# ScalarE's order during the residual update: embedding copies moved behind two tiles' act_hi

## The reference

```python
x = x + rmsnorm(y, norm_post[i])
gate = jax.nn.sigmoid(rmsnorm(x, pe_norm[i]) @ pe_w_gate[i])
x = x + gate * (p[i] @ pe_w_proj[i])
```

## Time and profile before

| | |
|---|---|
| median of 3 runs | 659.37 us |
| the profiled execution: its own time | 658.61 us |
| its span, first to last instruction | 656.8 us |
| TensorE busy | 635.0 us (97%) |
| VectorE, ScalarE, GpSimd busy | 389.9, 321.2, 308.1 us |
| chain that ended last | TensorE 81%, VectorE 9%, ScalarE 4% |
| mean granted clock of TensorE | 0.997 |

### The profile page before, as it was taken

One profiled execution on the slowest core, in us unless ns is written; L12 is line 12 of the kernel. 1 busy time (PEld: TensorE's weight loads), 2 busy tenths in 40 slices (PEclk: granted clock), 3 DMA queues, 4 the chain that ended last, 5 costly groups with the idle time before them and its releaser, 6 DMA issues.

```text
span 656.8 us, 9280 instructions
## 1 busy us (share of the span) xinstructions
PE 635.0 (97%) x2930; PEld 516.4 (79%) x2930; DVE 389.9 (59%) x776; ACT 321.2 (49%) x556; POOL 308.1 (47%) x412
## 2 busy tenths in 40 slices
PE   6979999999999999899989999999999999999897
PEld 3758888888888887788767778888888887887686
DVE  5528787867878787645678735333423343365864
ACT  6536575755656575465547633212222222465461
POOL 1765555556464445200277647547454752001770
PEclk9989999999999999999999999999999999999999
DMA  6253333332433333135002413232223232250041
GB/s 200 88 174 128 127 106 105 104 105 104 129 118 114 111 129 125 33 128 188 6 33 72 150 53 110 98 125 96 96 68 123 96 128 87 94 173 32 33 128 65
DMA packets 27161, 68.69 MB, mean 105 GB/s; under 512 B 3568, under 2 KB 10096, under 8 KB 27136
## 3 DMA queue, kind: packets, MB, share of 16 engines
q1 hardware_dynamic: 27136, 68.37, 31.6%
HBM read 66.23 MB, written 2.13 MB: 104 GB/s over the span
## 4 chain that ended last, share of the span: by engine, by line
PE 81%; DVE 9%; ACT 4%; issue 3%; DMA 2%; SPq 0%; DVEq 0%; ACTq 0%
PE ps_pj L1028 23%; PE ps_pj L1030 23%; PE ps_pj L1029 23%; PE ps_tr L1037 3%; DVE act_lo L918 2%; DMA w_raw<-in_weights 2%; PE ps_o L1141 1%; PE ps_o L1142 1%; DVE xT L914 1%; PE ps_sc L1111 1%; PE ps_sc L1109 1%; PE ps_tr L1028 1%; PE ps_tr L1030 1%; PE ps_tr L1029 1%; ACT logit L524 1%
## 5 line engine op out<-in xcount | busy, mean ns | idle before, releaser
L408 POOL TENSOR_TENSOR w_lo<-w_raw,w_hi 128x256 fp32r<-128x256 f32 x324 | 251.5, 809 | 138.5 <-ACT w_hi L468 128.3
L1028 PE MATMUL ps_pj<-act_hi,w_hi 128*128 128x512 f32 (+1 forms) x736 | 293.9, 399 | 5.5 <-DVE act_lo L918 4.4
L1030 PE MATMUL ps_pj<-act_hi,w_lo 128*128 128x512 f32 (+1 forms) x736 | 286.2, 389 | 0.0
L1029 PE MATMUL ps_pj<-act_lo,w_hi 128*128 128x512 f32 (+1 forms) x736 | 285.9, 388 | 0.0
L1028 PEld LDWEIGHTS ps_pj<-act_hi,w_hi 128*128 128x128 f32 x736 | 138.8, 189 | 37.2 <-DVE act_lo L918 7.9
L1030 PEld LDWEIGHTS ps_pj<-act_hi,w_lo 128*128 128x128 f32 x736 | 138.5, 188 | 29.3
L1029 PEld LDWEIGHTS ps_pj<-act_lo,w_hi 128*128 128x128 f32 x736 | 139.0, 189 | 24.9 <-issue 0.7
L468 ACT CAST w_hi<-w_raw 128x1024 fp32r<-128x1024 f32 x96 | 100.6, 1048 | 97.4 <-DMA w_raw<-in_weights 74.9
L443 POOL TENSOR_TENSOR acc<-acc,sq 128x512 f32<-128x512 f32 x14 | 21.4, 1525 | 118.5 <-ACT sq L616 117.6
L416 POOL TENSOR_TENSOR bias<-bias,future 128x128 f32<-128x128 f32 x64 | 34.0, 562 | 72.8 <-DMA bias<-negc_scratch 72.8
L524 ACT ACTIVATE logit<-logit,nmax 128x128 f32<-128x128 f32 (+1 forms) x64 | 36.1, 564 | 60.4 <-DVE nmax L763 60.2
(11 more groups left out here) (143 smaller groups left out, 724.8 us busy)
## 6 DMA issues: line engine op xcount, KB each, us to landing
w_raw<-in_weights SPq DMA_DIRECT2D x100, 512.0 KB, 3.4
bias<-negc_scratch SPq DMA_DIRECT2D x16, 256.0 KB, 7.4
bias<-negc_scratch SPq DMA_DIRECT2D x16, 192.0 KB, 6.1
xT<-in_xT SPq DMA_DIRECT2D x8, 256.0 KB, 5.5
bias<-negc_scratch SPq DMA_DIRECT2D x16, 128.0 KB, 4.8
out<-xT SPq DMA_DIRECT2D x7, 256.0 KB, 2.0
bias<-negc_scratch SPq DMA_DIRECT2D x16, 64.0 KB, 3.4
p_in<-in_pT SPq DMA_DIRECT2D x2, 512.0 KB, 4.5
```

Of the source, the lines that this page charges most:

```text
L408: last = nc.gpsimd.tensor_tensor(w_lo[place % RING][:, tiles], w_raw[stream(place) % RAW][:, tiles], w_hi[place % RING][:, tiles], ALU.sub ...
L1028: nc.tensor.matmul(out, w_h, a[0][:, k, tokens], start=k == first, stop=False)
L1029: nc.tensor.matmul(out, w_h, a[1][:, k, tokens], start=False, stop=False)
L1030: end = nc.tensor.matmul(out, w_l, a[0][:, k, tokens], start=False, stop=k == last)
```

## The change

The first copy of an embedding tile leaves its place ahead of the loop, and all four copies of a layer are placed by the table: tile 0 after act_hi 1, tile 1 after act_hi 2, tiles 2 and 3 after act_hi 3. The other engines' programs are as they were.

```diff
-PLE_COPY_AT = {0: [1], 1: [2, 3]}
+PLE_COPY_AT = {1: [0], 2: [1], 3: [2, 3]}
...
                     nc.scalar.copy(pleT[:, m, :], ps_pj[s % 2][:]).then_inc(pj_free[s % 2], 1)
 
-                ple_copy(0)
                 for m in range(KT):
                     act.wait_ge(x_new, 2 * KT * l + m + 1)
                     nc.scalar.activation(a_g[:, m, :], xT[:, m, :], ACT.Copy, scale=g_pe[:, l, m:m + 1]
```

## The result

The changed kernel takes 654.02 us (median of 4 runs, 652.78 to 654.84) against 659.35 (median of 4 runs of the kernel before, 658.58 to 660.58). The two medians are 5.3 us apart; the ratio estimated from the same runs is 0.9912 with a 95% interval of 0.9888 to 0.9936, which is 5.8 us less (4.2 to 7.4). Measured once more, the ratio is 0.9933 (0.9915 to 0.9951), 4.4 us less.

A forecast was written before the change was run, and what follows sets the result against it. Matmuls bound the kernel nearly everywhere; only the gate stage, where TensorE waits for VectorE's act_lo, had something to give. 2 x 2.1 = 4.2 us off the median of 659.37 gave 655.2 us, range 653.9 to 657.4.

The forecast's parts named there:

- Step 1: ScalarE: act_hi 0 and 1 go ahead at no cost, act_hi 0 at 317.22, copy 0 still at 319.36.
- Step 2: VectorE: act_lo 0 starts at 318.42 rather than 320.60, 2.18 us sooner.
- Step 3: GpSimd: additions start near 320.55, slowing VectorE; act_lo 1 takes 1.1 us, xT 3 1.0, ending at 323.15.
- late bound of 324.0: VectorE: end of xT 3 if act_lo 1 takes 1.78 us and xT 3 1.21, the whole early overlap paid.
- Step 4: PSUM banks: copies 2 and 3 free them later; first gate product at 324.55, 1.36 us later, second-bank stop gone.
- Step 5: act_lo 6 ends at 337.0 as TensorE reaches tile 6; TensorE ends at 341.25, gaining 2.1 us a layer.
- Step 6: Later stages: TensorE is full there, so the shift is passed on whole; 2 x 2.1 = 4.2 us.
- A: Banks cost more: xT 3 at 324.0, TensorE starts at 325.4; gain 1.5 us a layer, 656.4 us; chance 0.14.
- B: No gain: GpSimd slows VectorE to a 3.40 us pitch, act_lo 6 ends at 339.1 as before; 659 us; chance 0.07.
- C: Slower: VectorE's pitch reaches 3.65 us, act_lo 6 ends 1.3 us later than now; 662.0 us; chance 0.03.
- E: Edit without effect: act_hi 0 on ScalarE finds another hold than copy 0; 659.4 us; chance 0.02.
- Rival D: TensorE's clock: the new 1.3 us idle lowers it for 3 us, losing 1.5 us a layer; 658.2 us; chance 0.04.

The follow-up runs named there:

- experiment 5: Kernel before, with GpSimd's additions of squares cut to one of 512 columns (output not the reference's): ratio 0.9888, stage 26.42 us in both layers.
- experiment 7: Changed kernel with copy 2 ahead of act_hi 3 and GpSimd's additions cut to one of 512 columns: ratio 0.9901, stage 26.69 and 26.67 us.
- experiment 1: The changed kernel measured again without any edit: ratio 0.9933 to the kernel before, stage 27.70 and 27.65 us.
- experiment 4: Kernel before, with copy 0 left first, copy 1 behind act_hi 2, copies 2 and 3 behind act_hi 3: ratio 1.0077, stage 32.30 and 30.68 us.
- experiment 9: Kernel before's copy places, but squares behind ScalarE's last act_hi and additions on VectorE behind its last act_lo: ratio 0.9966, stage 28.07 and 28.44 us.
- experiment 3: Changed kernel with copy 0 behind act_hi 0, copy 1 behind act_hi 1, copies 2 and 3 behind act_hi 2: ratio 0.9937, stage 28.23 and 28.19 us.
- experiment 2: Changed kernel with copy 2 moved ahead of act_hi 3: ratio 0.9904 to the kernel before, stage 26.99 and 27.03 us.

## Why the prediction was wrong

The direction and the mechanism were right; the number was not. 655.2 us was forecast with a range of 653.9 to 657.4. The measured ratio, put on the median of 659.37, is 653.6 (652.0 to 655.2), 0.3 us below the range; the median of the changed kernel itself, 654.02, lies 0.1 us inside it.

Measured times are given 0.26 us less here, on the time axis of the trace before.

- Step 1 held: act_hi 0 at 317.28 (forecast 317.22), copy 0 at 319.31 (319.36).
- Step 2 held: act_lo 0 starts at 318.43 (318.42), 2.17 us sooner.
- Step 3: the first addition starts at 320.50 (320.55). act_lo 1 took 0.74 us, not 1.1, and xT 3 1.07, not 1.0. The sum is near: xT 3 ends at 322.86 instead of 323.15. The late bound of 324.0, which a rule of the Trainium skill was taken to give (GPSIMD Engine Reference, section 1), did not come about: act_lo 1 had started 0.09 us ahead of the addition (320.67 against 320.76) and ran at its undisturbed speed beside it. What the rule says of VectorE's instructions with two SBUF inputs is borne out by experiment 5: act_lo takes 0.75 us without the additions (1.22 beside the weight remainder), up to 1.79 with them.
- Step 4: the first gate product starts at 324.24 (324.55), as much sooner as xT 3 was, and the stop before the second bank is gone. The idle time ahead of it is 0.81 us as the profile counts it, where 1.2 to 1.4 was forecast.
- Step 5: act_lo 6 ends at 336.84 (337.0), the norm product comes at 341.15 (341.25). TensorE restarts once, with 0.3 us lost, and not twice with 0.1 each. The term of 2.1 us a layer measured 2.23.
- Step 6 held: both later stages are as full as before, and nothing gives the gain back.

So the sum of 4.2 us should have been 4.46, and the second measurement gives 4.4. Two steps failed. The first is a term of the sum: "I take 1.1 us for act_lo 1" in step 3. It measured 0.74. With xT 3 itself 0.07 us longer, that brought xT 3, copy 2 and the first gate product 0.3 us sooner; act_lo 2 to act_lo 6 (12.27 us from start to start, 12.16 forecast) gave 0.1 of it back, and the norm product came 0.10 us ahead of its forecast. The forecast's 343.38 - 341.25 = 2.13 had also been rounded down to 2.1. Together that is the 0.13 us a layer.

The second is the sum of the range: "with the 1 us by which medians of this kernel scatter, the range is 653.9 to 657.4". On the slow side the 1 us is there (656.4 + 1). On the fast side the forecast's own range ends at 654.3, and 654.3 - 1 is 653.3, not 653.9: only 0.4 us was taken off. With 653.3 the 653.6 would have lain inside. No run shows the 1 us as the right size either; the interval of the ratio alone was 1.6 us to either side. Up to the first norm product of layer 0's tail every kernel here runs the same instructions, and yet that product comes between 310.94 us (experiment 7) and 313.71 us (the changed kernel), while the stretch between the two residual updates stays within 250.69 to 251.18 us in all traces. So in the traces most of the scatter lies ahead of that product. That the remaining 1.3 us of the first measurement are scatter rests on the stage times and on experiment 1; which stretches of its other executions held it was not traced.

Two readings of the earlier trace rows in the prediction are off, without an effect on the sum: the shortest slowed act_lo is 1.22 us, not 1.28, and not only one reaches 1.78, since act_lo 6 and 7, taken there as 1.74 each, are 1.77 to 1.78 in the trace.

Of the rivals, A, B, C and E did not come about: act_hi 0 started at 317.28, xT 3 was early, not late, and the five pitches from act_lo 1 to act_lo 6 took 335.32 - 320.67 = 14.65 us, 2.93 each instead of 3.4 or more. Rival D did not strike the changed kernel, whose clock stayed at 1.00 after its idle of 0.81 us. Its reading, "the rows say that one of this size is not" a danger, does not hold, though. Experiment 4, with longer stops in the same stage, and experiment 9, with a stop ahead of the norm product, were struck. And in the attention of experiments 3 and 5, in code that the change does not touch, the clock fell after two idle times of 0.9 and 1.2 us. Experiment 3, TensorE, and the stretch behind it:

```profile
261.65 0.55 PE L1036 MATMUL ps_tr<-ident,logit 128*128 128x128 f32 x3 [0.90 <-DVE logit L771]
...
264.06 0.94 PE L1036 MATMUL ps_tr<-ident,logit 128*128 128x128 f32 x4 [1.17 <-DVE logit L771]
...
265.10:267.10 2.00, 2.00 (x8) 1.71 (x8) 1.34 (x6) 1.01 (x3) 0.17 (x1) 0.50 0.29 78
```

In experiment 1 the same two (0.89 and 1.16 us) left it at 1.00. That the changed kernel's stop of 0.81 us passed without it, in both layers of both traces, may in part be luck; the runs don't show which idle times it survives.

## What to carry to other kernels

Before work is moved ahead on an idle engine, find what makes the chain behind it slow: here VectorE lagged because GpSimd's additions ran beside it, and where they were cut short (experiment 5) the order of before had the shortest stage of all. An order change has two ends: each copy that moves back holds a bank, so follow every bank to the matmul that wants it next (experiment 4 missed one and was 5 us slower). And where a change is worth under 1%, time a stage between two fixed marks in several traces; it repeated within 0.05 us here between layers and between executions of one kernel (but for experiments 4 and 9, with the longest stops of TensorE), while whole runs differed by 2 us.

## What the runs showed of the hardware

- An act_lo of 128 x 512 takes 0.74 us alone and 1.22 to 1.79 us beside GpSimd, depending on how the two lie; one that starts just ahead of an addition still takes 0.74 (the changed kernel's act_lo 1). GpSimd's addition itself takes between 1.29 us (experiment 3) and 1.84 (the changed kernel). A gap of 0.9 us between two additions was worth 1.0 us to one instruction of VectorE (experiment 2).
- The granted clock fell to 0.50 after one stop of 1.84 us (experiment 9, layer 1) and after stops of 1.97 and 2.11 us (experiment 4, layer 0), but not after the same two stops in layer 1 of experiment 4, nor after 1.47 us in layer 0 of experiment 9. After idle times of 0.9 and 1.2 us it fell in experiments 3 and 5 and not in experiment 1. I had expected only idle times like the 4.13 us of the earlier trace rows to do so. At 0.50 the matmuls of experiment 4 start 0.43 us apart, at 1.00 0.23. The Trainium skill (TensorE: Matmul & The Clock Gate, part 1) says that the throttled clock is the default and that activity releases it. The runs agree as far as idleness brings the lower clock back, and they add that the same idleness does not always.
